# Softmax in one tile of five buffers, with wider lags between the engines and half of the scaling on VectorE

## The chip, the cores and the metric

One core of one Trainium2 chip runs the whole program. The metric is device time in microseconds (us) of one execution. Engine names: PE or TensorE (matmuls and transposes), DVE or VectorE, ACT or ScalarE, SP (DMA issue).

## The reference

One inference step of a two-layer decoder trunk, in fp32, on a prompt of 1024 tokens and a group of 8 samples of 4 new tokens each, with shared weights (model width 1024). Layer 0 is gated linear attention and a ConvFFN. Layer 1 is sliding-window attention (window 128, 16 query heads over 2 key/value heads of width 64, a relative bias per head, one sink per head) and a ConvFFN. Each sub-layer is `h = h + post_norm(f(pre_norm(h)))` with RMSNorm. The attention of layer 1, where the change lies, is

```
s = q @ k.T * 64**-0.5 + bias            # keys of this block and the one before, masked
m = max(max(s), sink)
p = exp(s - m)
denom = sum(p) + exp(sink - m)
o = (p / denom) @ v                      # then o @ w_o_b, the down projection of the stage
```

For the prompt it is computed in blocks of 128 queries against 256 keys. The samples attend to 128 cached keys and their new ones.

## The kernel before

All tokens are transposed: channels lie on the 128 partitions, tokens along the free axis. The 1056 columns are worked on in two halves, X = 0 with 512 columns and X = 1 with 512 prompt and 32 sample columns. Each fp32 product is made of three matmuls, on a rounded part (`hi`) and a remainder (`lo`) of the activations and of the weights. So each weight block of 128x1024 is rounded by ScalarE (L416), its remainder taken by VectorE (L421), in rings of three, and each new activation has a `hi` written by ScalarE and a `lo` by VectorE. SP loads the next raw block when a remainder has been taken.

The stages run one after the other, and within a stage each engine has an order written out by hand; engines meet by counted semaphores alone. The attention stage (`pe_att`, `dve_att`, `act_att`) loops over steps s. A step belongs to one iteration g: a pair of heads (q = g // 4: X and the pair) and one block of 128 queries. There are 64 iterations (NIT), and the loop also carries the rest of the stage, placed by `k, w = divmod(s, 8)`: query projections (`query`, half a block of weights in each of w = 0 to 3), the down projection of the pairs that are complete (`downs`, in w = 4 to 7, a quarter of its 8 or 16 units in each; a unit is the sum over two weight blocks into one of three banks, and VectorE adds it to the accumulator, L471 and L473), the samples' attention (the functions with `s_`, in k = 4 to 8), and two norms whose parts stand in tables by step (`PE_AT`, `DVE_AT`, `ACT_AT`: squares `sq`, folds `f`, the sum over partitions, the root, scaling `s`, residual `a`, then the normed rows `n` and their `hi` and `l`).

One iteration passes these functions, the step at which each engine runs it in brackets:

- `scores(g)` on TensorE [g]: two matmuls into banks 0 and 1. It waits until VectorE has read those of g - 1.
- `biased(g)` on VectorE [g]: adds the bias and finds the maximum with the sink, from the banks into `SS` (two buffers); for the first two of four blocks it also copies the sink's column (L1838).
- `exps(g)` on ScalarE [g]: two exponentials with their sums, from `SS` into `EX` (three buffers).
- `divided(g)` on VectorE [g + 1]: the reciprocal of the two sums.
- `scaled(g)` on ScalarE [g + 1]: two scalings in `EX` by the reciprocals (L1993).
- `transposed(g)` on TensorE [g + 2]: four transposes into bank 2. It waits until ScalarE has copied out those of g - 1.
- `turned(g)` on ScalarE [g + 2]: the copy from bank 2 into `PT` (L2003, L2006).
- `values(g)` on TensorE [g + 3]: the product with the values into a half of bank 4. For an even g it waits for `lo(g - 1)`; in the second half, for g % 8 == 2, also for the sample's new scores (`s_new`), which use the same bank.
- `hi(g)` and `lo(g)`, for an odd g, on ScalarE and VectorE [g + 4]: both blocks of bank 4 into `OH1` and `OL1`, the operands of `downs`.

Within a step the order is: TensorE `scores`, `transposed`, a query half or (w = 4 to 7) `downs` and `s_new`, `values`, `s_scores` and the like, a norm's sum. VectorE: `divided`, `lo`, `biased`, weight remainders, `adds`, the samples' work, the norm's work. ScalarE: `hi`, `scaled`, `exps`, `turned`, `query` (copies and a rounding), roundings, the samples' work, the next bias load, the norm's work. All engines work through their lists in order, so a wait holds everything behind it. A few lines that the prediction speaks of:

```
def biased(g):                                   # VectorE, before
    u, r = g % 2, g % 8
    ...
    dve.wait_ge(sf, g + 1)                       # scores(g)
    if g >= 2:
        dve.wait_ge(es, g - 1)                   # exps(g - 2) has read the buffer
```

Of the kernel before, what the change touches and what calls it, by code (L numbers as in the profile page):

```python
# [15 lines left out]
P = 128  # L16
# [152 lines left out]
def build(nc, wall, xT, gains, ffnpar, wgate, state, kcT, vc, ck, cv, onehot, masks, smask, bmask,  # L169
# [10 lines left out]
    with ctx:  # L180
# [11 lines left out]
        def sem(name):  # L192
# [68 lines left out]
        EX = place("probs", [P, 3, 2, NBW])  # L261
        SS = place("scores", [P, 2, 2, NBW])
# [88 lines left out]
        sn, sk, sf, sa, es, rc, sc = (sem("att_" + x) for x in ("sinks_negated", "sink", "scores", "biased", "exp", "rden", "scaled"))  # L351
        tf, te, of, xh, xl = (sem("att_" + x) for x in ("pt", "pt_copied", "o", "hi", "lo"))
        xsn, xsf, xsa, xsb, xex, xrc, xsc, xtf, xte, xof, xoh, xol = (
            sem("samp_" + x) for x in ("scores_new", "scores", "biased", "masked", "exp", "rden", "scaled", "pt", "pt_copied", "o", "hi", "lo"))
# [1222 lines left out]

        NIT, PAIRS, WINDOWS = 16 * HB, 16, 8
# [10 lines left out]
        def down_bank(k, m):  # L1589
# [8 lines left out]
        DVE_AT = {1: ("f0",), 2: ("f1",), 4: ("s0", "s1"), 5: ("a0", "s2"), 6: ("a1", "s3"), 7: ("a2",), 8: ("a3",), 9: ("F0",),  # L1598
# [4 lines left out]
        PE_AT = {3: "sum", 11: "Sum", 47: "sum", 55: "Sum"}  # L1603
        SUM_BANK = {3: 6, 11: 6, 47: 5, 55: 5}
# [3 lines left out]
        QUERY_DONE = {1: 2, 2: 6} | {q: 8 * ((q - 1) // 2) + (1 if q % 2 else 3) for q in range(3, PAIRS)}  # L1608
# [8 lines left out]
        def pe_att(pe):  # L1617
            def query(q, ks):
# [6 lines left out]
                for c in range(len(CHUNKS[X])):  # L1625
                    if ks[0] == 0 and q:
# [9 lines left out]
                        if q >= 11 and q % 2 and c == 0:  # L1636
                            pe.wait_ge(xsa, 3 * (k - 5) + 3)
                            if q >= 13:
                                pe.wait_ge(ms_done, NORMS[3, "post" if q == 13 else "pre", 0])
# [16 lines left out]
            def transposed(g):  # L1656
                X, q, i, blk, x0 = it_of(g)
                pe.wait_ge(sc, g + 1)
                if g:
                    pe.wait_ge(te, g)  # L1660
                for e in range(2):
                    for k in range(x0 // WIN, 2):
                        m = 2 * e + k
                        last = nc.tensor.transpose(PS[:, 2, m * P:(m + 1) * P], EX[:, g % 3, e, k * WIN:(k + 1) * WIN],
                                                   ident[:])
                last.then_inc(tf, 1)

            def values(g):
                X, q, i, blk, x0 = it_of(g)
                pe.wait_ge(te, g + 1)  # L1670
                if g >= 2 and g % 2 == 0:
                    pe.wait_ge(xl, g // 2)
                    if X and g % 8 == 2:
                        pe.wait_ge(xsa, 3 * (g // 8 - 4) + 1)
# [7 lines left out]
            def downs(k, units):  # L1682
# [3 lines left out]
                if units[0] == 0:  # L1686
# [7 lines left out]
                    else:  # L1694
                        pe.wait_ge(q_ev, AQ[1, min(2 * k - 4, 7), 1])
                for m in units:
# [27 lines left out]
            def s_scores(d, half):  # L1724
                if half:
                    pe.wait_ge(xsa, 3 * d + 2)
# [46 lines left out]
            for s in range(NIT + 4):  # L1773
                k, w = divmod(s, 8)
# [5 lines left out]
                if 2 <= s < NIT + 2:  # L1780
                    transposed(s - 2)
                if k == 0:
                    if w in FIRST_QUERIES:
                        query(*FIRST_QUERIES[w])
                elif w < 2 and k < 8:
                    query(2 * k + 1, (FIRST, SECOND)[w])
                elif w < 4 and k < 7:
# [747 lines left out]
```

## Time and profile before

| | |
|---|---|
| time, median of 3 runs (lowest, highest) | 2627.01 us (2624.51, 2628.49) |
| profiled execution: time, span | 2624.26 us, 2622.5 us |
| mean granted clock of TensorE | 0.983 of full speed |
| instructions | 37815 |
| DMA traffic over the span | 255.18 MB, mean 97 GB/s |

The busy time of an engine is the time in which at least one of its instructions ran. A wait is idle time of an engine before an instruction, put down to the instruction whose semaphore came last; "out<-in" are the program's tile names, and the line is that of the kernel (or of a helper that several places share, as L438 for all projections and L461 for all down projections). The granted clock is a share of full speed: 1.00 stands for 2.4 GHz, and a stretch below it was for a part at 1.2 GHz. The attention stage's first scores start at 1415.17 us, its last (g = 63) at 1783.42 us.

### The profile page before, as it was taken

The page shows a single profiled execution, that of the slowest core. Times are in us where ns is not written, and L with a number is a line of the kernel's source. Part 1 is how long each engine was busy: PE and PEld are TensorE (multiplying, and loading weights), DVE is VectorE, ACT ScalarE, POOL GpSimd, SP SyncE. Part 2 cuts the span into 40 slices and gives each one's busy share as a digit, 9 for nine tenths or more (in the row PEclk, how much of TensorE's full clock was granted, in tenths as well). Part 3 has the DMA queues.
Part 4 walks back from the last instruction along what each step waited for, and adds up shares of the span by engine and source line. Part 5 has one row for each costly group of instructions (what it writes and reads, how often), then busy time and mean ns, then how long its engine had stood idle before and what let it go on. Part 6 is the DMA issues. An engine that isn't in the chain of part 4 may idle for free. (4 is left out here: it accounts for less than half of the span.)

```text
span 2622.5 us, 37815 instructions
## 1 busy us (share of the span) xinstructions
PE 2485.6 (95%) x15455; PEld 2177.1 (83%) x15455; DVE 1619.1 (62%) x2921; ACT 1147.4 (44%) x1810; POOL 0.2 (0%) x4
## 2 busy tenths in 40 slices
PE   7999999999999999999998899989999999999997
PEld 4777989887788889999997676767788889999996
DVE  5677566576666556666655755665666556655556
ACT  4655454453443333343334766663434334332333
POOL 0000000000000000000000000000000000000000
PEclk9999999999999999999999999999999999999998
DMA  4222223223433333322233332231343333332322
GB/s 156 65 73 73 81 84 106 89 91 103 142 113 105 108 99 105 121 93 86 89 95 99 98 97 67 89 100 52 106 139 97 97 96 96 114 113 81 92 86 96
DMA packets 93433, 255.18 MB, mean 97 GB/s; under 512 B 12499, under 2 KB 43708, under 8 KB 91324
## 3 DMA queue, kind: packets, MB, share of 16 engines
q1 hardware_dynamic: 63884, 202.43, 24.4%
q10 hardware_dynamic: 29376, 50.33, 5.8%
q8 instruction: 123, 2.02, 0.3%
q14 instruction: 50, 0.41, 0.1%
HBM read 225.92 MB, written 26.74 MB: 96 GB/s over the span
## 5 line engine op out<-in xcount | busy, mean ns | idle before, releaser
L438 PE MATMUL banks<-act_hi,w_lo 128*128 128x272 f32 (+1 forms) x2952 | 975.0, 330 | 16.8 <-DVE act_lo L2262 7.5
L438 PE MATMUL banks<-act_hi,w_hi 128*128 128x272 f32 (+1 forms) x2952 | 960.9, 326 | 0.0
L438 PE MATMUL banks<-act_lo,w_hi 128*128 128x272 f32 (+1 forms) x2952 | 959.3, 325 | 0.0
L416 ACT ACTIVATE w_hi<-w_raw 128x1024 fp32r<-128x1024 f32 x366 | 380.7, 1055 | 698.3 <-PE banks L461 490.9
L421 DVE TENSOR_TENSOR w_lo<-w_raw,w_hi 128x1024 fp32r<-128x1024 f32 x366 | 442.6, 1223 | 366.3 <-ACT w_hi L416 366.0
L438 PEld LDWEIGHTS banks<-act_hi,w_lo 128*128 128x128 f32 x2952 | 560.2, 190 | 75.2 <-issue 21.3
L438 PEld LDWEIGHTS banks<-act_lo,w_hi 128*128 128x128 f32 x2952 | 561.1, 190 | 43.0 <-issue 1.7
L438 PEld LDWEIGHTS banks<-act_hi,w_hi 128*128 128x128 f32 x2952 | 559.5, 190 | 43.6
L473 DVE TENSOR_TENSOR acc<-acc,banks 128x272 f32<-128x272 f32 (+1 forms) x624 | 315.0, 520 | 191.7 <-PE banks L461 188.2
L461 PE MATMUL banks<-h_hi,w_lo 128*128 128x272 f32 (+1 forms) x1056 | 348.1, 330 | 30.0 <-DVE acc L473 13.1
L461 PE MATMUL banks<-h_hi,w_hi 128*128 128x272 f32 (+1 forms) x1056 | 345.7, 327 | 0.0
L461 PE MATMUL banks<-h_lo,w_hi 128*128 128x272 f32 (+1 forms) x1056 | 345.6, 327 | 0.0
L461 PEld LDWEIGHTS banks<-h_hi,w_lo 128*128 128x128 f32 x1056 | 200.6, 190 | 52.8 <-DVE acc L473 17.3
L461 PEld LDWEIGHTS banks<-h_lo,w_hi 128*128 128x128 f32 x1056 | 202.1, 191 | 16.7
L461 PEld LDWEIGHTS banks<-h_hi,w_hi 128*128 128x128 f32 x1056 | 200.8, 190 | 15.8
L1499 ACT ACTIVATE u<-banks 128x512 f32<-128x512 f32 (+2 forms) x132 | 59.6, 452 | 201.4 <-PE banks L438 198.5
L1513 ACT ACTIVATE c<-u,par 128x512 f32<-128x512 f32 (+1 forms) x88 | 73.1, 830 | 71.0 <-issue 67.9
L1421 DVE SCALAR_TENSOR_TENSOR c<-u,par,c 128x512 f32<-128x512 f32 (+1 forms) x88 | 68.2, 775 | 46.7 <-ACT c L1513 46.7
L1389 DVE TENSOR_TENSOR h_lo<-hf,h_hi 128x512 fp32r<-128x512 f32 (+1 forms) x88 | 62.1, 706 | 34.8 <-ACT h_hi L1554 34.8
L1554 ACT ACTIVATE h_hi<-hf 128x512 fp32r<-128x512 f32 (+1 forms) x88 | 56.0, 637 | 57.5 <-DVE hf L1447 29.9
L461 PE MATMUL banks<-o_hi,w_lo 128*128 128x272 f32 (+1 forms) x192 | 66.6, 347 | 13.4 <-DVE acc L473 8.2
L1845 DVE CUSTOM_DVE_ANT_0 scores<-banks,bias,sinks_b 128x256 f32<-128x256 f32 (+1 forms) x128 | 54.5, 464 | 37.1 <-PE banks L1652 21.9
(231 smaller groups left out, 2591.1 us busy)
## 6 DMA issues: line engine op xcount, KB each, us to landing
w_raw<-wall SPq DMA_DIRECT2D x366, 512.0 KB, 3.6
normed<-h_scratch ACTq DMA_DIRECT2D x20, 352.0 KB, 3.7
h_scratch<-acc ACTq DMA_DIRECT2D x3, 2176.0 KB, 7.6
h_scratch<-acc ACTq DMA_DIRECT2D x3, 2048.0 KB, 8.3
gstates<-state ACTq DMA_DIRECT2D x4, 1024.0 KB, 6.3
gla_s<-gstates ACTq DMA_DIRECT2D x4, 1024.0 KB, 6.6
bias<-bias_scratch ACTq DMA_DIRECT2D x28, 128.0 KB, 2.3
bias_scratch<-bias_rows ACTq DMA_DIRECT2D x8, 383.0 KB
```

The lines of the kernel that those rows point to most:

```text
L416: nc.scalar.activation(WH[:, b % RING], WR[:, b % RAW], ACT.Copy).then_inc(w_hi, 1)
L421: nc.vector.tensor_tensor(WL[:, b % RING], WR[:, b % RAW], WH[:, b % RING].bitcast(fp32), ALU.subtract).then_inc(w_lo, 1)
L438: last = nc.tensor.matmul(PS[:, bank, 0:n], w, a[X][:, k, o:o + n], start=(k == 0 and first), stop=(k == KT - 1 and w is wh and a is AH))
L461: last = nc.tensor.matmul(PS[:, bank, 0:w_], w, a[t][:, o:o + w_], start=(t == 0 and x == 0), stop=(t == 1 and x == 2))
L473: nc.vector.tensor_tensor(a, a, PS[:, bank, 0:w_], ALU.add).then_inc(dn_add, 1)
L1389: nc.vector.tensor_tensor(HL[:, t % 2, 0:W], HF[:, t % 2, 0:W], HH[:, t % 2, 0:W].bitcast(fp32), ALU.subtract).then_inc(hl, 1)
L1421: nc.vector.scalar_tensor_tensor(C[:, 0:cv], U[:, 1:1 + cv], PAR[:, t, 17:18], C[:, 0:cv], ALU.mult, ALU.add).then_inc(cv1, 1)
L1499: last = nc.scalar.activation(U[:, 2 + o:2 + end], PS[:, bank, 0:end - o], ACT.Copy)
L1513: nc.scalar.activation(C[:, 0:cv], U[:, 2:2 + cv], ACT.Identity, bias=PAR[:, t, 19:20], scale=PAR[:, t, 18:19]).then_inc(cb, 1)
L1554: nc.scalar.activation(HH[:, t % 2, 0:WX[X]], HF[:, t % 2, 0:WX[X]], ACT.Copy).then_inc(hh, 1)
L1845: last = nc.vector.tensor_tensor_reduce(SS[:, u, e, x0:2 * WIN], PS[:, e, x0:2 * WIN], BI[:, q % 2, e, x0:], -1.0, SINK[:, 2 * (q % 8) + e ...
```

## The change

The score and probability tiles become one tile `SE` with five buffers; the exponentials and scalings work in place. The lags grow: on ScalarE `exps` at g + 1, `scaled` at g + 3, `turned` at g + 4; on VectorE `divided` at g + 2; on TensorE `transposed` at g + 4, `values` at g + 5; `hi` and `lo` at g + 6. `divided` also scales the second head's probabilities on VectorE, so `scaled` keeps only the first. The sink's column is copied for each iteration (its buffer is now overwritten by the exponential). `k, w` are counted from s - 1. On TensorE `values` and `s_new` come before `downs`, whose units are spread 1, 3, 2, 2 (X = 0) and 2, 5, 4, 5 (X = 1) over the four steps. On VectorE `divided` comes behind `biased`, and `s_new` is one step later. The norm tables move, the sums of the second norm use bank 3, and the first projection of the next layer is cut differently. The semaphore of the sample's biased scores is split in two.

```diff
-        EX = place("probs", [P, 3, 2, NBW])
-        SS = place("scores", [P, 2, 2, NBW])
+        SE = place("scores", [P, 5, 2, NBW])
...
         ACT_AT = {0: ("sq0",), 1: ("sq1",), 2: ("h0", "h1"), 3: ("root",), 5: ("h2",), 6: ("h3",), 8: ("Sq0",), 9: ("Sq1",),
-                  11: ("Root",), 12: ("hi0",), 14: ("hi1",),
-                  38: ("sq0",), 39: ("sq1",), 41: ("h0", "h1"), 47: ("root",), 50: ("h2",), 51: ("h3",), 52: ("Sq0",), 53: ("Sq1",),
-                  55: ("Root",), 57: ("hi0",), 60: ("hi1",)}
+                  11: ("Root",), 12: ("hi0",), 15: ("hi1",),
+                  39: ("sq0",), 40: ("sq1",), 42: ("h0", "h1"), 43: ("root",), 46: ("h2",), 47: ("h3",), 51: ("Sq0",),
+                  53: ("Sq1",), 57: ("Root",), 58: ("hi0",), 60: ("hi1",)}
...
-                  10: ("F1",), 12: ("n0a", "n0b"), 13: ("l0a", "l0b"), 14: ("n1a", "n1b"), 15: ("l1a", "l1b"),
-                  39: ("f0",), 40: ("f1",), 48: ("s0",), 49: ("s1",), 50: ("a0", "s2"), 51: ("a1", "s3"), 52: ("a2", "a3"),
-                  53: ("F0",), 54: ("F1",), 56: ("n0a",), 57: ("n0b",), 58: ("l0a", "l0b"), 59: ("n1a",), 60: ("n1b",),
-                  61: ("l1a",), 62: ("l1b",)}
-        PE_AT = {3: "sum", 11: "Sum", 47: "sum", 55: "Sum"}
-        SUM_BANK = {3: 6, 11: 6, 47: 5, 55: 5}
+                  10: ("F1",), 12: ("n0a", "n0b"), 13: ("l0a", "l0b"), 15: ("n1a", "n1b"), 16: ("l1a", "l1b"),
+                  40: ("f0",), 41: ("f1",), 44: ("s0", "s1"), 45: ("a0",), 46: ("a1",), 48: ("s2",), 49: ("s3",),
+                  50: ("a2", "a3"), 52: ("F0",), 54: ("F1",), 58: ("n0a", "n0b"), 59: ("l0a", "l0b"),
+                  60: ("n1a", "n1b"), 61: ("l1a",), 62: ("l1b",)}
+        PE_AT = {3: "sum", 11: "Sum", 43: "sum", 57: "Sum"}
+        SUM_BANK = {3: 6, 11: 6, 43: 3, 57: 3}
...
+        UNITS = ((0, 1, 4, 6, 8), (0, 2, 7, 11, 16))
...
-            for s in range(NIT + 4):
-                k, w = divmod(s, 8)
+            for s in range(NIT + 5):
+                k, w = divmod(s - 1, 8)
...
-                if 2 <= s < NIT + 2:
-                    transposed(s - 2)
+                if 4 <= s < NIT + 4:
+                    transposed(s - 4)
...
+                if w == 5 and 0 <= d < 4:
+                    s_new(d)
+                if 5 <= s < NIT + 5:
+                    values(s - 5)
                 if w >= 4 and 1 <= k < 8:
-                    units = len(down_units((k - 1) // 4)) // 4
-                    downs(k - 1, range((w - 4) * units, (w - 3) * units))
-                if d >= 0 and w == 4 and d < 4:
-                    s_new(d)
-                if 3 <= s < NIT + 3:
-                    values(s - 3)
+                    downs(k - 1, units_at(k - 1, w))
...
             def biased(g):
-                u, r = g % 2, g % 8
-                if i < 2:
-                    if g >= 2:
-                        dve.wait_ge(es, g - 1)
-                    p = q % 8
-                    nc.vector.tensor_copy(SS[:, u, :, 2 * WIN:NBW], SINK[:, 2 * p:2 * p + 2].unsqueeze(2)).then_inc(sk, 1)
+                u, r, p = g % 5, g % 8, q % 8
+                if g >= 5:
+                    dve.wait_ge(tf, g - 4)
+                else:
+                    dve.wait_ge(sf, g + 1)
+                nc.vector.tensor_copy(SE[:, u, :, 2 * WIN:NBW], SINK[:, 2 * p:2 * p + 2].unsqueeze(2)).then_inc(sk, 1)
...
                 nc.vector.reciprocal(ST[:, g % 8, 6:8], ST[:, g % 8, 4:6]).then_inc(rc, 1)
+                dve.wait_ge(rc, g + 1)
+                x = SE[:, g % 5, 1, x0:2 * WIN]
+                nc.vector.tensor_scalar(x, x, ST[:, g % 8, 7:8], None, ALU.mult).then_inc(sc1, 1)
...
-                for e in range(2):
-                    x = EX[:, g % 3, e, x0:2 * WIN]
-                    last = nc.scalar.activation(x, x, ACT.Copy, scale=ST[:, g % 8, 6 + e:7 + e])
-                last.then_inc(sc, 1)
+                x = SE[:, g % 5, 0, x0:2 * WIN]
+                nc.scalar.activation(x, x, ACT.Copy, scale=ST[:, g % 8, 6:7]).then_inc(sc, 1)
...
-                if s >= 4 and s % 2 == 1:
-                    hi(s - 4)
+                if s >= 7 and s % 2:
+                    hi(s - 6)
                 if 1 <= s <= NIT:
-                    scaled(s - 1)
-                if s < NIT:
-                    exps(s)
-                if 2 <= s < NIT + 2:
-                    turned(s - 2)
+                    exps(s - 1)
+                if 3 <= s < NIT + 3:
+                    scaled(s - 3)
+                if 4 <= s < NIT + 4:
+                    turned(s - 4)
```

## Rows read from the trace of the kernel before

**Rows 1.** The page's first part: busy time and share of each engine.
```profile
...
PE 2485.6 (95%) x15455; PEld 2177.1 (83%) x15455; DVE 1619.1 (62%) x2921; ACT 1147.4 (44%) x1810; POOL 0.2 (0%) x4
...
```

**Rows 2.** Busy time by stretch: stretch, length, each engine's busy us, granted clock.
```profile
...
1415.00:1499.00 84.00, 64.05 (x356) 43.81 (x356) 56.04 (x140) 62.57 (x135) 0.00 (x0) 0.96 0.31 101
1499.00:1593.00 94.00, 88.24 (x553) 68.43 (x555) 53.38 (x138) 58.48 (x152) 0.00 (x0) 0.96 0.34 96
1593.00:1812.00 219.00, 198.32 (x1511) 156.63 (x1508) 129.26 (x353) 137.21 (x332) 0.00 (x0) 0.97 0.24 75
...
```

**Rows 3.** Waits of TensorE, 1400 to 1805 us: total us, times, longest.
```profile
...
PE banks L1664 <- ACT probs_t L2006: 14.4, 11, 2.8
PE banks L461 <- DVE acc L473: 8.3, 6, 2.8
PE banks L1678 <- DVE o_lo L1859: 7.4, 5, 2.5
PE banks L1678 <- DVE s_scores L1874: 3.3, 4, 1.0
PE banks L461 <- DVE w_lo L421: 3.2, 2, 1.8
...
PE banks L1664 <- ACT probs_t L2003: 2.6, 1, 2.6
...
```

**Rows 4.** Busy time by 10 us stretch; the third last column is the clock.
```profile
...
1440.00:1450.00 10.00, 7.75 (x43) 5.27 (x43) 9.72 (x22) 7.52 (x25) 0.00 (x0) 0.83 0.30 82
...
1790.00:1800.00 10.00, 10.00 (x61) 7.77 (x61) 4.20 (x8) 5.47 (x10) 0.00 (x0) 0.83 0.33 106
...
```

**Rows 5.** Timeline of all engines, step 13 of the stage: start us, us.
```profile
...
1478.87 2.86 DVE L568 SCALAR_TENSOR_TENSOR normed<-acc,gain_cols,rstd 128x544 f32<-128x544 f32 x4
...
1479.38 0.66 PE L1664 MATMUL banks<-ident,probs 128*128 128x128 f32 x4
...
1481.77 2.02 ACT L578 ACTIVATE act_hi<-normed 128x2176 fp32r<-128x2176 f32 x1 [2.79 <-DVE normed L568]
...
1483.69 0.36 ACT L2015 ACTIVATE o_hi<-banks 128x256 fp32r<-128x256 f32 x1
...
1484.09 0.42 DVE L1859 TENSOR_TENSOR o_lo<-banks,o_hi 128x256 fp32r<-128x256 f32 x1 [2.28 <-ACT o_hi L2015]
...
1484.66 0.66 PE L1678 MATMUL banks<-probs_t,v_tok 128*64 128x128 f32 x8 [1.82 <-DVE o_lo L1859]
...
```

**Rows 6.** Timeline of all engines, step 37 of the stage.
```profile
...
1617.85 0.70 PE L1652 MATMUL banks<-kg,q 64*128 64x256 f32 x4
...
1618.60 0.48 DVE L1845 CUSTOM_DVE_ANT_0 scores<-banks,bias,sinks_b 128x256 f32<-128x256 f32 x1 [0.71 <-PE banks L1652]
...
1622.57 0.18 DVE L1874 TENSOR_TENSOR s_scores<-banks,s_bias 128x32 f32<-128x32 f32 x1
1622.66 0.68 DVE L1880 TENSOR_TENSOR s_scores<-banks,s_bias 128x512 f32<-128x512 f32 x1
...
1622.90 0.66 PE L1678 MATMUL banks<-probs_t,v_tok 128*64 128x128 f32 x8 [0.97 <-DVE s_scores L1874]
...
1623.49 1.07 PE L1732 MATMUL banks<-kcg,q_sample 64*64 64x512 f32 x4
...
```

**Rows 7.** Groups by shape, 1405 to 1800 us: busy us, mean ns | idle.
```profile
...
L1993 ACT ACTIVATE probs<-probs,stats 128x256 f32<-128x256 f32 x112 | 50.5, 500 | 27.0 <-DVE stats L1852 24.1 <-issue 2.8
L1845 DVE CUSTOM_DVE_ANT_0 scores<-banks,bias,sinks_b 128x256 f32<-128x256 f32 x112 | 49.5, 480 | 27.6 <-PE banks L1652 21.9 <-issue 5.7
...
L416 ACT ACTIVATE w_hi<-w_raw 128x1024 fp32r<-128x1024 f32 x33 | 33.9, 1051 | 11.7 <-PE banks L461 11.7
...
L1852 DVE RECIPROCAL stats<-stats 128x2 f32<-128x2 f32 x64 | 10.3, 160 | 16.3 <-ACT probs L1984 16.1
...
```

**Rows 8.** Timeline of VectorE in the sample's scaling.
```profile
...
1637.65 0.17 DVE L1898 RECIPROCAL s_stats<-s_stats 128x1 f32<-128x1 f32 x1
1637.86 0.77 DVE L1900 TENSOR_SCALAR s_scores<-s_scores,s_stats 128x1056 f32<-128x1056 f32 x1
...
```

More of the change, by code:

```diff
@@ L1663, in transposed @@
                         m = 2 * e + k
-                        last = nc.tensor.transpose(PS[:, 2, m * P:(m + 1) * P], EX[:, g % 3, e, k * WIN:(k + 1) * WIN],
+                        last = nc.tensor.transpose(PS[:, 2, m * P:(m + 1) * P], SE[:, g % 5, e, k * WIN:(k + 1) * WIN],
                                                    ident[:])
@@ L1695, in downs @@
                         pe.wait_ge(q_ev, AQ[1, min(2 * k - 4, 7), 1])
+                    if k in (4, 6):
+                        pe.wait_ge(ms_done, NORMS[3, "post" if k == 4 else "pre", 0])
                 for m in units:
@@ L1814, in pe_att @@
                     pe.wait_ge(sa, NIT)
-                elif s == NIT + 2:
+                elif s == NIT + 4:
                     pe.wait_ge(te, NIT)
-                if s >= NIT:
-                    pe_first_block(pe, 2, "u" if w < 2 else "val", (FIRST, SECOND)[w % 2])
+                    pe_first_block(pe, 2, "val", ALL)
+                if NIT <= s < NIT + 4:
+                    pe_first_block(pe, 2, "u", range(2 * (s - NIT), 2 * (s - NIT) + 2))
             downs(7, range(len(down_units(1))))
@@ L1908, in s_lo @@
                 last.then_inc(xol, 1)
-            for s in range(NIT + 4):
-                k, w = divmod(s, 8)
+            for s in range(NIT + 6):
+                k, w = divmod(s - 1, 8)
                 d = k - 4
-                if 1 <= s <= NIT:
-                    divided(s - 1)
-                if s >= 4 and s % 2 == 1:
-                    lo(s - 4)
+                if s >= 7 and s % 2:
+                    lo(s - 6)
                 if s < NIT:
                     biased(s)
+                if 2 <= s < NIT + 2:
+                    divided(s - 2)
+                if w == 6 and 0 <= d < 4:
+                    s_new(d)
                 for q in range(1, PAIRS):
@@ L1923, in dve_att @@
                     rest_after(dve, ("kv", 1, w // 2 - 1))
-                elif w == 0 and k >= 2:
-                    for t in range(2):
-                        rest_after(dve, ("ao", (k - 2) // 4, (k - 2) % 4, t))
+                elif w < 2 and k >= 2:
+                    rest_after(dve, ("ao", (k - 2) // 4, (k - 2) % 4, w))
                 if w >= 4 and 1 <= k < 8:
-                    units = len(down_units((k - 1) // 4)) // 4
-                    adds(k - 1, range((w - 4) * units, (w - 3) * units))
+                    adds(k - 1, units_at(k - 1, w))
                 if d >= 0:
@@ L2064, in act_att @@
             act.wait_ge(cn_out, 16)
-            for s in range(NIT + 4):
-                k, w = divmod(s, 8)
+            for s in range(NIT + 6):
+                k, w = divmod(s - 1, 8)
                 d = k - 4
-                if s >= 4 and s % 2 == 1:
-                    hi(s - 4)
+                if s >= 7 and s % 2:
+                    hi(s - 6)
                 if 1 <= s <= NIT:
-                    scaled(s - 1)
-                if s < NIT:
-                    exps(s)
-                if 2 <= s < NIT + 2:
-                    turned(s - 2)
+                    exps(s - 1)
[3 more added lines that the diff above has]
+                    turned(s - 4)
                 for q in range(1, PAIRS):
@@ L2078, in act_att @@
                         query(q)
-                if w == 7 and k:
+                if w == 7 and k > 0:
                     downs_done(k - 1)
@@ L2096, in act_att @@
                         act_step(act, *pass_at(s), name, SUM_BANK.get(s))
-                if s in (20, 23):
-                    act_hi(act, 2, "mix", 1, (s - 20) // 3)
+                if s in (21, 24):
+                    act_hi(act, 2, "mix", 1, (s - 21) // 3)
             for what in ("u", "val"):
```

71 lines of the change are left out of this document (36 added, 35 removed).

## The prediction

> **What bounds the kernel now.** I read the page's first part, then the busy time by stretch, the waits of TensorE, the durations by shape, and the timelines around three waits. TensorE is busy for 95% of the span [rows 1], so outside the attention stage there is nothing for this change to win. The change touches one stage, from about 1415 us to 1812 us. There TensorE is busy for 64.1 of 84, 88.2 of 94 and 198.3 of 219 us [rows 2]: 350.6 of 397 us, so about 46 us of idle time. VectorE is busy for 238.7 us and ScalarE for 258.3 us of the same 397 us. No engine is full, and the idle time of TensorE comes from hand-overs. The reader should see by name what those 46 us are [rows 3]: 14.4 + 2.6 us before a transpose that waits until ScalarE has copied the previous block's transposed probabilities out of the one bank; 8.3 us before a down-projection unit that waits for VectorE's accumulation; 3.2 us for a weight remainder; 7.4 us before the value product that waits for VectorE's `lo` of the pair before; 3.3 us before the value product that waits for the sample's new scores. That is 39.2 us. The clock is the other loss: there are eight dips of it in the stage, each like the 10 us stretches at a granted clock of 0.83, the first from 1440 and the last from 1790 [rows 4]. In each, TensorE was at the lower level (1.2 GHz) for part of the stretch after having waited, and a 10 us stretch at 0.83 does 1.7 us less work. What lies in those stretches is partly hidden behind the other engines.
>
> **The change part by part.** All sums are against the profiled execution's own time, 2624.3 us (a span of 2622.5 us and 1.8 us around it); the median of the runs shown is 2.8 us above it, and I add that at the end.
>
> *Later transposes and no same-step exponentials (first term).* Before, ScalarE's copy in a step stands behind that step's exponentials, which stand behind VectorE's biased scores, which stand behind TensorE's scores of the same step. After, exponentials lag by one step, the scaling by three, the copy by four. That removes the ping-pong of 17.0 us [rows 3] where nothing else holds ScalarE. It does not remove it where ScalarE sits in the norm's squares, its root or its 2.02 us `act_hi` [rows 5], because the transpose of one step still needs the copy of the step before, at the same distance as now. The longest of these waits are such ones. I let 5 us go; the ends are 0 and 17.
>
> *Units spread 1, 3, 2, 2 and 2, 5, 4, 5, and the second norm's residual work spread over more steps (second term).* The 8.3 + 3.2 us before down-projection units arise where VectorE is behind in its queue. Fewer units in the first of the four steps and less norm work beside them let most of it go. The sample's masking stays where it was. I take 8 us off; the ends are 0 and 11.5.
>
> *The value product moves ahead of the down-projection units (third term, the largest).* In a step with units the order on TensorE was scores, transposes, units, values; it becomes scores, transposes, values, units. The value product of an even block waits for `lo` of the odd block before it, which comes from `hi` on ScalarE, which comes from the value product one step earlier. The lag is wider, but `hi` and `lo` are shifted so that they stay in the step of that value product. Until now units covered the hand-over. Without them TensorE reaches the values after at most 0.70 us of scores [rows 6] and 0.66 us of transposes [rows 5]; the two overlap a little, and I reckon 1.05 to 1.3 us. In the first step with units ScalarE first finishes the query that ended just before, whose copies are followed by a weight rounding of 1.051 us [rows 7]; then come `hi` 0.36 us and `lo` 0.42 us [rows 5]. That is 1.8 us, the copies and two hand-overs beside it. The stall is an estimated 1 to 2 us; it appears in three windows (in the later ones the sample's value products lie in between): 5 us. It is worse behind `act_hi`. In step 13 of the kernel before, the chain normed 2.86 us, `act_hi` 2.02 us, `hi`, `lo` ended 1.82 us after TensorE was ready, although two units had just run [rows 5]. Those two units would now stand behind the wait; they filled the time from the transposes at 1479.38, 0.66 us long, to 1482.84, where the wait began: 2.8 us. So such a place costs about 4.6 us, and there are three: steps 13, 59 and 61, since `act_hi` is placed in 12, 58 and 60. That makes 14 us, with 5 us above and about 1.5 us elsewhere, against 7.4 us now: +13 us. The ends are −7 (all of it hidden) and +18.
>
> *The sample's new scores one step later (fourth term).* VectorE's add now stands behind the biased scores and the scaling of the same step, and TensorE's value product of that step waits for it. From the start of TensorE's scores VectorE begins 0.75 us later [rows 6], needs some 0.9 us for its two biased rows of 0.48 us [rows 7] (they overlap a little), about 0.5 us for reciprocal and scaling (below) and 0.18 us for the add: 2.4 us with the hand-over. TensorE is there after 1.05 to 1.3 us. So 1.1 to 1.4 us in each of four windows, 5.3 us against 3.3 us now [rows 3]: +2 us, ends −3.3 and +5.
>
> *The second half of the sample scores (fifth term).* It waits for VectorE's 0.68 us add of the first half. Now the value product lies between [rows 6]: the add begins at 1622.66, the second half starts at 1623.49, right behind the values. When the values are gone from there, TensorE waits through the accumulation of the last unit and that add, 1.3 to 1.5 us, four times: +5.5 us, ends 0 and +6.
>
> *The second head's scaling on VectorE (sixth term).* ScalarE loses 56 operations of 0.500 us and 8 shorter ones [rows 7], some 30 us of its time. VectorE gains 64 scalings. The trace has none of this shape; the nearest rows are the 1056-wide one at 0.77 us [rows 8] and the two-column reciprocal at 0.160 us [rows 7], which are the ends, and a line through both gives 0.31 us, the value I take. In front of it VectorE waits for its own reciprocal: in the sample's chain the scaling starts 0.21 us behind the reciprocal's start [rows 8]. With 32 more two-column sink copies (each about the 0.160 us of the reciprocal) VectorE gets 64 × 0.31 + 32 × 0.16 = 25 us more, 264 of 397 us: hidden behind TensorE as a whole. Where VectorE leads, in the first steps, it is not: +1.5 us, ends 0 and +6. What queues behind that new wait is the rest of VectorE's step: weight remainders, accumulations, norm work. The scaling in place and the shared tile change no shape.
>
> *Edits at nothing.* The first projection of the next layer in four quarters and then whole is the same work in the drain, where its matmuls cover the longer tail of transposes and values. The sums' new bank and the split semaphores add no instruction on a path. The weight queue follows VectorE's remainders by the same wait as now, and ScalarE's rounding never waited for a load in this stage (the 11.7 us of idle time in its row are TensorE's) [rows 7].
>
> The sum: −5 − 8 + 13 + 2 + 5.5 + 1.5 = +9 us, with the clock's dips left at eight. On the profiled execution that is 2633.3 us; with the 2.8 us to the median, **2636 us**, slower by 0.34%. A change under about 0.2%, 5.3 us, can't be told from none by measuring this kernel.
>
> **Rivals.** *The lag works (faster).* ScalarE idles 27.0 us before the scalings alone [rows 7], because they wait within the step. Relieved of half of them and with every input a step old, it may run ahead, so that `hi` starts the moment the value product ends. The rival decides where `hi`, `lo` and two hand-overs, about 1 us, fit under scores and transposes, 1.05 to 1.3 us as above. Then the third to fifth terms come to about zero, the first to −12 and the second to −9: 2624.3 − 21 + 2.8 = 2606 us. For it: the gap is that narrow. Against it: the query's rounding stands ahead of `hi` on ScalarE.
>
> *The waits trade places (no change).* If VectorE's norm chain ends some 3 us earlier than now at each of the three places, the third term falls from +13 to about +4 and the sum to 0: 2627 us. For it: the first norm's root is no longer behind exponentials of its own step. Against it: the chain starts with squares that wait for VectorE, which has more to do.
>
> *The clock follows the waits (slower still).* About nine of the new stalls are over 1 us long. If each is answered by one more stretch like those in [rows 4], 1.7 us apiece, the time is 2636 + 15 = 2651 us. Against it: of some thirty waits now only eight are followed by a dip. The Trainium skill, "TensorE: Matmul & The Clock Gate", section "HAM oscillation — how this bites in real kernels", describes a kernel whose bursts of matmuls each start cold after a wait, and says that the transition cost is paid for every burst instead of once. By that rule this rival would hold; the trace agrees only in part, with dips behind eight of the waits.
>
> **How the numbers follow.** The forecast gets 0.36, with a range of its own from 2632.5 to 2643 us; the faster rival 0.33; no change 0.22; the clock 0.09. Cases of both signs hold most of the chance, so the full range reaches from 2602 to 2653 us: a little below the faster rival, where the first term gives more, and just above the clock's. Faster by over 0.2%: 0.33. Within: 0.22. Slower: 0.36 + 0.09 = 0.45.
>
> **What would show it.** In the profile after, the waits of value products for `lo` should grow from 7.4 to about 20 us, above all at steps 13, 59 and 61; those for the sample's scores to 5 us, with a new one of 5 us at the second half. Waits for transposed probabilities should fall only to about 12 us and those for accumulations to 3 or 4 us. VectorE's busy time should rise by 20 to 30 us, ScalarE's fall by 26 to 31 us. The forecast is wrong if value products hardly wait; then the faster rival stands.

## The result, and the profile after

The changed kernel takes 2636.5 us (median of 9 runs, 2630.9 to 2639.1) against 2624.5 us of the kernel before (9 runs, 2620.5 to 2629.5): a ratio of 1.004 with an interval of 1.003 to 1.005. The forecast was 2636 us. Its profiled execution took 2631.8 us, a span of 2629.9 us. The first part of the page, answering to [rows 1]:

```profile
PE 2488.9 (95%) x15455; PEld 2176.6 (83%) x15455; DVE 1642.5 (62%) x3017; ACT 1119.8 (43%) x1746; POOL 0.2 (0%) x4
```

VectorE gained 23.4 us of work, ScalarE lost 27.6 us, and TensorE has as many matmuls as before. What changed is when TensorE waits. Its waits from 1400 to 1840 us, answering to [rows 3] (total us, times, longest):

```profile
PE banks L1686 <- DVE o_lo L1870: 23.9, 12, 4.9
PE banks L1672 <- ACT probs_t L2011: 5.6, 2, 3.3
PE banks L1686 <- DVE s_scores L1885: 5.4, 4, 2.2
PE banks L1742 <- DVE s_scores L1891: 4.8, 4, 1.4
...
PE banks L1672 <- ACT probs_t L2014: 2.8, 1, 2.8
PE banks L461 <- DVE w_lo L421: 2.0, 1, 2.0
...
PE banks L461 <- DVE acc L473: 1.3, 3, 0.6
PE banks L461 <- DVE acc L471: 0.2, 1, 0.2
```

The reader should see two groups. The waits that were large in [rows 3], for `probs_t` and `acc`, are small. In their place stands one row, `o_lo`, 7.4 us before and 23.9 us now, with two smaller ones for the sample's scores. The view of before has one more wait for `acc`, which the prediction did not count:

```profile
PE banks L461 <- DVE acc L471: 2.1, 1, 2.1
```

Step 13 shows how the wait for `o_lo` comes about (timeline of all engines, answering to [rows 5]):

```profile
1465.13 2.87 DVE L568 SCALAR_TENSOR_TENSOR normed<-acc,gain_cols,rstd 128x544 f32<-128x544 f32 x4 [1.08 <-ACT rstd L523]
...
1467.12 0.66 PE L1672 MATMUL banks<-ident,scores 128*128 128x128 f32 x4
...
1468.07 2.01 ACT L578 ACTIVATE act_hi<-normed 128x2176 fp32r<-128x2176 f32 x1
1469.98 0.37 ACT L2023 ACTIVATE o_hi<-banks 128x256 fp32r<-128x256 f32 x1
...
1470.38 0.43 DVE L1870 TENSOR_TENSOR o_lo<-banks,o_hi 128x256 fp32r<-128x256 f32 x1 [2.38 <-ACT o_hi L2023]
...
1470.95 0.69 PE L1686 MATMUL banks<-probs_t,v_tok 128*64 128x128 f32 x4 [3.18 <-DVE o_lo L1870]
```

TensorE has nothing to do after the transposes of 1467.12 until `lo` is there: `hi` stands behind the 2.01 us of `act_hi` on ScalarE. The down units, which filled that time before, come after the values (e1 below shows what they would do in this place now).

The whole stage, from the first scores to the last down unit's matmul, in both kernels (busy time by stretch: length, busy us of each engine, granted clock). First before, then after:

```profile
1415.17:1822.88 407.71, 360.83 (x2496) 279.02 (x2495) 245.68 (x644) 258.27 (x617) 0.00 (x0) 0.97 0.27 84
```

```profile
1409.41:1831.07 421.66, 368.99 (x2496) 283.73 (x2495) 269.42 (x740) 230.66 (x553) 0.00 (x0) 0.95 0.26 81
```

The stage is 14.0 us longer. TensorE's idle time in it rose by 5.8 us, from 46.9 to 52.7, and its busy time by 8.2 us although the matmuls are the same: the granted clock fell from 0.97 to 0.95. Summed over windows of 1 us, TensorE stood at the lower level (1.2 GHz) for 27.3 us before and 40.9 us after; half of the difference, 6.8 us, is about what the lost speed costs. The lowest stretches, answering to [rows 4] (10 us each):

```profile
1440.00:1450.00 10.00, 7.16 (x38) 5.08 (x38) 7.57 (x22) 6.75 (x20) 0.00 (x0) 0.66 0.70 244
...
1470.00:1480.00 10.00, 9.05 (x37) 6.10 (x38) 7.89 (x20) 5.75 (x20) 0.00 (x0) 0.66 0.19 54
1770.00:1780.00 10.00, 7.36 (x44) 5.16 (x44) 4.95 (x18) 5.87 (x14) 0.00 (x0) 0.66 0.01 2
```

The last two hold the ends of the waits of step 13 (at 1470.95) and step 61 (at 1772.64). (The execution as a whole is only 7.6 us longer than the one before, because its stage began 5.8 us earlier. Nothing ahead of the stage was changed, and the stage begins anywhere from 1409.4 to 1418.5 us in the fourteen profiled executions of this study.)

### The profile page after: what moved, and what is told of

Same layout as the page of the kernel before. It is cut to its first block and busy times, and to the rows that moved or that the text cites. A ratio compares the mean times of both kernels' runs of the same rounds, so it can differ in the third digit from the quotient of the medians.

```text
span 2629.9 us, 37807 instructions
## 1 busy us (share of the span) xinstructions
PE 2488.9 (95%) x15455; PEld 2176.6 (83%) x15455; DVE 1642.5 (62%) x3017; ACT 1119.8 (43%) x1746; POOL 0.2 (0%) x4
## 5 line engine op out<-in xcount | busy, mean ns | idle before, releaser
L438 PE MATMUL banks<-act_hi,w_lo 128*128 128x272 f32 (+1 forms) x2952 | 975.3, 330 | 16.3 <-DVE act_lo L2271 7.1
L461 PE MATMUL banks<-go_hi,w_lo 128*128 128x272 f32 (+1 forms) x192 | 62.7, 326 | 9.2 <-issue 6.0
```

The costliest lines, as they stand in the source:

```text
L438: last = nc.tensor.matmul(PS[:, bank, 0:n], w, a[X][:, k, o:o + n], start=(k == 0 and first), stop=(k == KT - 1 and w is wh and a is AH))
L461: last = nc.tensor.matmul(PS[:, bank, 0:w_], w, a[t][:, o:o + w_], start=(t == 0 and x == 0), stop=(t == 1 and x == 2))
```

## The experiments

All are timed in five rounds beside the kernel before, whose median was 2624.9 to 2625.2 us in them. The stage, idle time and low clock are of each one's profiled execution, measured as above. One execution can lie well off its kernel's median: e4's took 2644.8 us, the changed kernel's 2631.8 and e15's 2613.3.

| kernel | median us | ratio to before (interval) | stage us | TensorE idle us | at 1.2 GHz us |
|---|---|---|---|---|---|
| before | 2624.5 | 1 | 407.7 | 46.9 | 27.3 |
| after | 2636.5 | 1.004 (1.003 to 1.005) | 421.7 | 52.7 | 40.9 |
| e1 values late | 2623.5 | 0.9997 (0.9986 to 1.0007) | 407.5 | 42.8 | 37.6 |
| e2 scaling on ScalarE | 2640.1 | 1.006 (1.0048 to 1.0072) | 426.0 | 53.8 | 47.8 |
| e3 sample's add early | 2634.8 | 1.0036 (1.0024 to 1.0048) | 420.8 | 49.0 | 47.8 |
| e4 `act_hi` later | 2637.0 | 1.0051 (1.0038 to 1.0065) | 425.7 | 54.6 | 44.4 |
| e5 = e1 + e3 | 2621.5 | 0.9988 (0.9975 to 1.0001) | 404.9 | 41.9 | 34.1 |
| e7 even units | 2639.4 | 1.0061 (1.0042 to 1.0081) | 424.7 | 54.5 | 41.0 |
| e8 `lo` a step earlier | 2651.0 | 1.0109 (1.0083 to 1.0135) | 434.3 | 61.3 | 51.2 |
| e9 = e8 + sample early | 2639.7 | 1.0059 (1.0039 to 1.0079) | 425.5 | 51.2 | 58.1 |
| e12 before, values early | 2665.8 | 1.0148 (1.0119 to 1.0176) | 451.5 | 73.9 | 68.3 |
| e13 old residual pass | 2641.1 | 1.0063 (1.0038 to 1.0089) | 426.1 | 56.7 | 37.6 |
| e14 = e5 + old pass | 2620.4 | 0.9976 (0.9962 to 0.999) | 406.0 | 40.1 | 37.6 |
| e15 = e14 + scaling on ScalarE | 2620.4 | 0.9982 (0.997 to 0.9994) | 403.5 | 41.4 | 27.3 |

**e1, values behind the down units again.**

```diff
-                if 5 <= s < NIT + 5:
-                    values(s - 5)
                 if w >= 4 and 1 <= k < 8:
                     downs(k - 1, units_at(k - 1, w))
+                if 5 <= s < NIT + 5:
+                    values(s - 5)
```

> The changed kernel with values(s - 5) behind the down units again in TensorE's step; all else stays. Theory (the waits for lo are what the change bought with its new order, 23.9 us of them at L1686): the down units of the step, 3.5 to 7 us, stand before values again, so the waits for o_lo fall to about 8 us, the waits for the new scores' addition (5.4 us) lie behind the down units too and go, and the clock loses fewer low stretches; the time falls 15 to 20 us below the changed kernel, to 2617 to 2622 us, some 5 us below the kernel before. Rival 'VectorE's scaling delays lo': the waits stay at 16 us or more and the time stays within 4 us of 2636.5. Rival 'waits trade places': the waits for accumulations, gone in the changed kernel, come back with 8 us or more, and the time falls by less than 10 us.

Measured: 2623.5 us, 13 us under the changed kernel, where 15 to 20 were expected, and the same as the kernel before. The mechanism is the theory's only in part. Its waits (same view):

```profile
PE banks L461 <- issue: 14.1, 6, 5.0
PE banks L1686 <- DVE o_lo L1870: 6.0, 4, 3.7
...
PE banks L1742 <- DVE s_scores L1891: 2.4, 4, 0.8
...
```

`o_lo` fell to 6.0 us, and the waits of 5.4 us for the new scores are gone, as foretold. But 14.1 us appeared at the down units, put down to "issue". Step 13 in e1's timeline tells what that is:

```profile
1476.42 0.37 ACT L2023 ACTIVATE o_hi<-banks 128x256 fp32r<-128x256 f32 x1
...
1476.82 0.42 DVE L1870 TENSOR_TENSOR o_lo<-banks,o_hi 128x256 fp32r<-128x256 f32 x1 [2.38 <-ACT o_hi L2023]
...
1477.45 0.47 PE L461 MATMUL banks<-o_hi,w_lo 128*128 128x512 f32 x1 [3.24 <-issue]
```

The unit starts 0.21 us behind the end of `lo`, and so do the other five of these waits (0.21 to 0.24 us). The code says why: `downs(k - 1, ...)` begins with a wait for `xl` up to 4k, that is `lo(8k - 1)`. That `lo` is now taken in step 8k + 5, in which the units begin; before it was taken in step 8k + 3 and the units began in 8k + 4. So in the first step with units the units can cover nothing: they ask for the same `lo`. This was not in the prediction. Of 23.9 us the order gives back 3.8 (6.0 + 14.1 remain); the new scores' 5.4 and half of the second half's 4.8 go as well. With other waits a little longer TensorE idles 9.9 us less, and its busy time in the stage is 4.3 us shorter, of which 1.7 us are half of the 3.3 us less at the lower level. So of the order's 13 us `lo` is the smaller part.

**e12, the new order alone.** In the kernel before, values and the sample's new scores move ahead of the units; VectorE's add of the new scores moves ahead of its accumulations.

```diff
+                if d >= 0 and w == 4 and d < 4:
+                    s_new(d)
+                if 3 <= s < NIT + 3:
+                    values(s - 3)
                 if w >= 4 and 1 <= k < 8:
                     ...
-                if d >= 0 and w == 4 and d < 4:
-                    s_new(d)
-                if 3 <= s < NIT + 3:
-                    values(s - 3)
```

> The kernel before with one thing of the change alone: TensorE's values (and the sample's new scores) stand ahead of the down units; VectorE takes the new scores ahead of its adds, without which this order could not run. Theory (the order of values and down units is what cost the 13 us, whatever the lag and the buffers): the waits for o_lo rise from 7.4 to 14 to 20 us, the new scores' addition from 3.3 to about 5, and the time from 2625 to 2632 to 2640. Rival 'the lag of two steps is the cause, the order matters only with it': o_lo stays under 10 us and the time within 3 us of 2625. Rival 'values early bring the next step's lo and copies forward': the waits for probs_t and the accumulation fall by 5 us or more, and the time falls.

Measured: 2665.8 us, 41 us over before, far more than expected. Its waits:

```profile
PE banks L1678 <- DVE o_lo L1859: 34.5, 10, 5.9
PE banks L1664 <- ACT probs_t L2007: 9.4, 6, 2.5
PE banks L1678 <- DVE s_scores L1874: 8.9, 4, 4.3
PE banks L1732 <- DVE s_scores L1880: 4.8, 4, 1.4
...
```

Here the order alone takes the wait for `lo` from 7.4 to 34.5 us. The stage grew by 43.7 us: 27.0 of idle time and 16.7 of busy time, where half of the 41.0 us more at the lower level would be 20.5. The order costs 41 us without the rest of the change and 13 us with it. So the rest (buffers, lags, units, norm tables and scaling together) wins some 28 us where values stand early, and nothing that can be told where they stand late (e1 against before: 0.9997).

**e8, `hi` and `lo` at the end of the values' own step.** If `lo` is late because it starts a step after its values, starting it earlier should help.

```diff
-                if s >= 7 and s % 2:
-                    lo(s - 6)
 ...
+                if s >= 6 and s % 2 == 0:
+                    lo(s - 5)
                 if w >= 4 and 1 <= k < 8:
                     adds(k - 1, units_at(k - 1, w))
```

The same for `hi` on ScalarE, behind the query's copies.

> The changed kernel with hi and lo of a pair of queries taken at the end of the step in which TensorE makes the pair's second values (hi(s - 5) on ScalarE behind the step's copies, lo(s - 5) on VectorE ahead of the adds), and not at the start of the next; all else stays, values ahead of the down units too. Theory (lo is taken one step after its values, behind whatever the residual's pieces leave on ScalarE and VectorE, and both the next values and the group's first down units ask for it in that same step): the waits for o_lo fall from 23.9 to 6 us or less, the first down units wait for nothing, the long low stretches of the clock at the first and last residual passes shrink, and the time falls by 18 to 26 us, to 2610 to 2619. Rival 'ScalarE and VectorE now stand still in line': both wait for TensorE's values inside the step, so the probabilities and the accumulators come later; the waits for probs_t, stats and acc rise by 10 us or more and the time stays above 2630. Rival 'only the order on TensorE counts': waits move, time within 4 us of 2636.5.

Measured: 2651.0 us, 14 us slower. The first rival holds:

```profile
PE banks L1672 <- ACT probs_t L2014: 12.2, 6, 2.8
PE banks L1659 <- DVE stats L1852: 10.5, 7, 2.8
PE banks L461 <- DVE acc L473: 7.7, 4, 3.7
PE banks L1686 <- DVE o_lo L1870: 5.3, 5, 1.5
...
PE banks L461 <- DVE acc L471: 3.5, 2, 2.9
...
```

`o_lo` fell to 5.3 us as expected, and other waits rose by more: `probs_t` from 8.4 to 16.3 us (with the 4.1 us of another row), `stats` from 3.7 to 10.5, `acc` from 1.5 to 11.2. VectorE itself now stands idle for 79.6 us before `lo`, waiting for `hi`, against 51.8 us in the changed kernel, and what is queued behind `lo` is late. Taking `lo` earlier only chooses another victim.

**e4, `act_hi` later.** `hi0` in steps 13 and 59 instead of 12 and 58, the last `hi1` in 61, their `lo` pieces a step later.

```diff
-                  11: ("Root",), 12: ("hi0",), 15: ("hi1",),
+                  11: ("Root",), 13: ("hi0",), 15: ("hi1",),
 ...
-                  53: ("Sq1",), 57: ("Root",), 58: ("hi0",), 60: ("hi1",)}
+                  53: ("Sq1",), 57: ("Root",), 59: ("hi0",), 61: ("hi1",)}
```

> The changed kernel with the residual's hi0 taken one step later (13 and 59), the last layer's hi1 at 61, and their lo steps one step later with them, so that ScalarE does no 2-us residual piece in the steps 12 and 58 to 60 in which hi and the sums' copies are due for lo. Theory (the three long waits of values at steps 13, 59 and 61, 11.8 us together, come of the residual's act_hi of 2 us ahead of o_hi on ScalarE): two of the three at least fall under 1.5 us, o_lo's waits from 23.9 to 14 to 17 us, and the time falls by 6 to 10 us, to 2626 to 2631. Rival 'lo is late everywhere': the long waits move to other steps (15, 61, 63) with the piece, the sum stays above 21 us and the time within 2 us of 2636.5.

Measured: 2637.0 us; `o_lo` 22.1 us. The waits at 13 and 59 fell, 3.18 to 1.29 and 3.70 to 1.91 us, but 2.39 us came up at step 15, and step 61 stayed at 5 us with another cause (its timeline):

```profile
1782.05 2.74 DVE L568 SCALAR_TENSOR_TENSOR normed<-acc,gain_cols,rstd 128x512 f32<-128x512 f32 x4
...
1784.71 0.42 DVE L1870 TENSOR_TENSOR o_lo<-banks,o_hi 128x256 fp32r<-128x256 f32 x1
1784.82 1.91 ACT L578 ACTIVATE act_hi<-normed 128x2048 fp32r<-128x2048 f32 x1 [3.34 <-DVE normed L568]
...
1785.27 1.13 PE L1686 MATMUL banks<-probs_t,v_tok 128*64 128x128 f32 x8 [5.01 <-DVE o_lo L1870]
```

Now VectorE's own norm holds `lo`, and `act_hi` comes after. The rival is right; the theory, that `act_hi` alone makes the wait, is not. (The edit has a part in step 61: its later `lo` pieces of the norm stand ahead of the norm's rows in step 60 on VectorE.)

**e3, the sample's first add ahead of the accumulations**; **e5, that with e1**; and **e9, that with e8, and the new scores' add right behind `lo` in w = 5 (before: in w = 6).**

```diff
+                if w == 5 and d >= 0:
+                    s_add(d, 0)
                 if w >= 4 and 1 <= k < 8:
                     adds(k - 1, units_at(k - 1, w))
 ...
-                    elif w == 5:
-                        s_add(d, 0)
```

> The changed kernel with s_add(d, 0) ahead of the down units' adds in VectorE's steps w = 5; all else stays. Theory (the second half of the sample's scores waits for an addition that is queued behind the adds): the four waits at L1742 go from 1.1 to 1.4 us each to under 0.3, 4.8 us to 1 us or less, and the time falls by 3 to 5 us, to 2631 to 2634. Rival 'the wait moves on': the adds come 0.6 us later, and lo or the accumulations of the same steps wait by as much; the time stays within 1.5 us of 2636.5.

Measured: 2634.8 us. The waits at L1742 are gone (4.8 us), those for the new scores rose by 1.0 and for `o_lo` by 0.9, and TensorE idles 3.7 us less. The median fell by 1.7 us, which the intervals do not separate from nothing.

> The changed kernel with values behind the down units (as in e1) and s_add(d, 0) ahead of the adds (as in e3). Theory (what is left at L1742 with values late, 2.4 us in e1, goes, and nothing takes its place): 1 to 3 us under e1's 2623.5, so 2620.5 to 2622.5; the waits of the first down units for lo (13 us) stay as in e1. Rival: the same as e1 within 1 us.

Measured: 2621.5 us, 2.0 under e1, with overlapping intervals. The waits at L1742 are gone here too; those for `o_lo` at the values rose from 6.0 to 7.6 us.

> As e8, and VectorE takes the sample's new scores (s_new) right behind that lo in step w = 5 and the first half of the sample's scores (s_add(d, 0)) ahead of the adds. Theory: beside what e8 gives, the 5.4 us at L1686 for s_scores and the 4.8 us at L1742 go to 1.5 us or less together; 7 to 9 us under e8, so 2602 to 2611. Rival 'the waits move on': the adds and lo come later by what was moved ahead of them, the accumulation waits rise by as much, and the time is within 3 us of e8's.

Measured: 2639.7 us, 11.2 us under e8 (intervals apart). Both kinds of sample waits are gone from the view, 5.0 + 4.8 us in e8, and the others stayed within 2 us of e8's. So these two waits do cost what they last, in this pair; the absolute forecast failed with e8's.

**e7, even units.** 

```diff
-        UNITS = ((0, 1, 4, 6, 8), (0, 2, 7, 11, 16))
+        UNITS = ((0, 2, 4, 6, 8), (0, 4, 8, 12, 16))
```

> The changed kernel with the down units spread evenly over their four steps (2, 2, 2, 2 and 4, 4, 4, 4 in place of 1, 3, 2, 2 and 2, 5, 4, 5), which is the spread of the kernel before. Theory (term 2 of the prediction: the uneven spread takes away the waits for the accumulation): the accumulation's waits (L473, L471) rise from 1.5 to 6 to 11 us and the time by 4 to 9 us, to 2640 to 2646. Rival 'it was the residual's spread, not the units'': the accumulation's waits stay under 3 us, and the time stays within 2 us of 2636.5. Rival 'a longer first portion covers lo' is excluded by the order, since values stand ahead of the units.

Measured: 2639.4 us, not separable from the changed kernel. The accumulation's waits are 1.3 + 0.2 us as in it. The uneven spread is not what took them away.

**e13, the second residual pass placed as before**, and **e14, that with e5.**

```diff
-        PE_AT = {3: "sum", 11: "Sum", 43: "sum", 57: "Sum"}
+        PE_AT = {3: "sum", 11: "Sum", 48: "sum", 56: "Sum"}
```

ScalarE's and VectorE's pieces of that pass go with it, and the wait for the bank's reader goes back from the units to the query.

> The changed kernel with the second residual pass (steps 39 to 63) placed as in the kernel before, each piece one step later than there because the steps are counted from 1 now, its two sums in the bank of the sample's scores again. Theory (term 2: the pass's new spread, and not the down units', takes away the waits for the accumulation): the accumulation's waits rise from 1.5 to 6 us or more, the time to 2640 to 2646. Rival 'the new spread makes the long waits': the pieces that stand ahead of o_hi in steps 58 and 60 (act_hi 1.9 us, normed 2.7 us) are split, the waits for o_lo at steps 59 and 61 fall from 8.6 to 5 us or less, and the time falls by 3 to 6 us, to 2630 to 2634.

Measured: 2641.1 us. Both sides are in its waits:

```profile
PE banks L1688 <- DVE o_lo L1870: 17.0, 12, 3.2
PE banks L1688 <- DVE s_scores L1885: 7.0, 4, 3.8
...
PE banks L461 <- DVE acc L473: 5.1, 4, 2.8
...
PE banks L438 <- ACT rstd L521: 4.2, 2, 2.1
...
```

`acc` rose by 3.8 us and 4.2 us for the root came back; `o_lo` fell by 6.9, at steps 59 and 61 from 8.6 to 3.4. The pass's spread moves waits about and gains nothing that shows.

> As e13, but with values behind the down units and s_add(d, 0) ahead of the adds (as in e5). Theory of term 2: 3 to 8 us over e5's 2621.5, so 2625 to 2630, with the accumulation's waits back. Rival as in e13: the first down units' wait at step 61 (5.0 us in e1 and e5) and o_lo's at 59 (3.7) fall by 4 us together, and the time falls to 2616 to 2619, under both kernels.

Measured: 2620.4 us, 1.1 under e5, not separable from it; the ratio lies below 1 with its whole interval. Against e5, the 5.0 us wait of step 61 became 1.3 and the 3.7 us of step 59 2.2; `acc` is at 5.9 us and the root at 2.6.

**e2, both heads' scaling on ScalarE**, and **e15, the same in e14.**

```diff
-                x = SE[:, g % 5, 0, x0:2 * WIN]
-                nc.scalar.activation(x, x, ACT.Copy, scale=ST[:, g % 8, 6:7]).then_inc(sc, 1)
+                for e in range(2):
+                    x = SE[:, g % 5, e, x0:2 * WIN]
+                    last = nc.scalar.activation(x, x, ACT.Copy, scale=ST[:, g % 8, 6 + e:7 + e])
+                last.then_inc(sc, 1)
```

VectorE's scaling goes, and with it TensorE's wait for it.

> The changed kernel with both heads' probabilities scaled by ScalarE (as before the change); VectorE does the reciprocal alone. Theory (the scaling stands beside the bound, and its place is not what costs): VectorE's busy time falls by about 23 us, ScalarE's rises by about 27, the waits for o_lo stay between 19 and 26 us, and the time stays within 3 us of the changed kernel's 2636.5. Rival 'VectorE is the bound at the waits': o_lo's and the sample scores' waits fall by 8 us or more together and the time by 8 to 12 us, to about 2626. Rival 'ScalarE had no room': the transposes wait for the scaling again, 8 us more of L1672, and the time rises by 5 to 10.

Measured: 2640.1 us; VectorE's busy time 21.8 us lower, ScalarE's 23.7 higher, `o_lo` 24.0 us as in the changed kernel. The medians differ by 3.6 us, but the intervals of the two ratios just overlap.

> As e14, but ScalarE scales both heads' probabilities again (as in e2). Theory (VectorE's scaling is a gain of some 3 us by itself, as e2's 2640.1 against 2636.5 suggests, since ScalarE's 0.4 to 0.5 us less a step bring the probabilities earlier): 2 to 5 us over e14's 2620.4, so 2622 to 2625, with the waits for probs_t up by 2 us or more. Rival 'the scaling's place is worth nothing': within 1.5 us of e14. Rival of the prediction's term 6 (VectorE's 25 us more of work delay the adds and cost 1.5 us): 1 to 2 us under e14.

Measured: 2620.4 us, the same as e14. Where the scaling is done is worth nothing there that shows; in the changed kernel VectorE's scaling may be a gain of some 3 us, which is not shown.

## Why the prediction was right

The time was right, and so was the largest term, to 3.5 us; of its reasons only a part was. By its steps, on the two profiled executions:

- *First term* (−5): the waits of transposes for the copy fell from 17.0 us to 8.4 (5.6 + 2.8): −8.6. No run takes the lags alone away, so that they did it is argued and not shown.
- *Second term* (−8): the waits before the units were 11.5 us by the prediction's two rows [rows 3], and 13.6 with the 2.1 us of L471 that it left out; they became 3.5: −10.1. Of its two reasons e7 excludes the units' spread, and e13, the residual's old place, brings back 3.8 us of accumulation waits. The rest is not explained by a run.
- *Third term* (+13): 7.4 to 23.9 us: +16.5. Steps 13, 59 and 61 waited 3.2, 3.7 and 4.9 us, against 4.6 us foretold; the others came to 12.1 us, where 6.5 us were reckoned. The size is about right, but the reason given, that the units no longer cover the hand-over, accounts for little of it. With the units in front again (e1), 20.1 of the 23.9 us remain: 6.0 at the values, and 14.1 at the group's first units, which ask for the same `lo` in the same step and wait as long as the values had waited there. So against the kernel before, 12.7 of the 16.5 us come with the rest of the change and 3.8 with the order. In the kernel before, where the units did cover it, the order alone makes +27.1 us (e12). Either edit takes the cover away; the prediction saw one of them, and that its sum still fits is luck. Step 59 was listed for the wrong reason: it has no units in either kernel, and e1 keeps its 3.7 us. And e4 shows that `act_hi` is not the one cause: the norm's pieces on both engines delay whatever is queued behind them.
- *Fourth and fifth term* (+2 and +5.5): +2.1 (3.3 to 5.4) and 4.8 from nearly nothing. In e9 removing both was worth 11 us beside e8; in the changed kernel removing the fifth alone gave 1.7 us, not separable from nothing (e3).
- *Sixth term* (+1.5): the scaling took 0.355 us, where 0.31 was estimated, and VectorE gained 23.4 us for 25. A cost is not shown: moving it back gave +3.6 us (e2) and 0.0 (e15).

```profile
L1863 DVE TENSOR_SCALAR scores<-scores,stats 128x256 f32<-128x256 f32 x56 | 19.9, 355 | 2.0
```

That is the group by shape after, from 1400 to 1820 us (busy us, mean ns, idle ahead of it), the row that the kernel before did not have.

- *The clock* (left at eight dips): in the profiled executions the dips are nine, three of them twice as long as the others, and some 7 to 8 of the stage's 14.0 us are theirs (half of the low time 6.8, all of the busy time 8.2). That term, put at nothing, was mis-sized, and it is the rival "the clock follows the waits" at half its price. One execution says little here, though: e14 and e15 have the same median, and their profiled executions, of 2623.0 and 2613.3 us, had 37.6 and 27.3 us of low clock. Over the six kernels that keep the change's order with `lo` in place (after, e2, e3, e4, e7, e13) idle time is 53.5 us on average, low clock 43.3 and the stage 424.2; over the five with values late (before, e1, e5, e14, e15) 42.6, 32.8 and 405.9. Of the 18.3 us between them 10.9 are waits and about 5 are clock by the half of the low time; some 2 are not accounted for. The Trainium skill, "TensorE: Matmul & The Clock Gate", section "HAM oscillation — how this bites in real kernels", describes a kernel in which every burst after a wait pays the transition again; here the rows agree in direction, but not for each wait: the changed kernel has 35 waits in the whole of the view above and nine dips.

So of the foretold waits, −5 − 8 + 13 + 2 + 5.5 = +7.5 us, +4.7 us came (−8.6 − 10.1 + 16.5 + 2.1 + 4.8), the errors of the first two terms and the third cancelling in part. With waits that the prediction did not price, such as 1.5 us for a copy of the query (L1978), TensorE's idle time rose by 5.8 us; its busy time rose by 8.2 us, where the prediction had nothing, and the two make the stage's 14.0. Between the medians the difference is 12.0 us, where 9 were foretold; that 2636 met 2636.5 so closely is luck, since these 3 us are made up for by the median of before, which over 9 runs came out 2.5 us below the 2627.0 us that the forecast was built on.

The rival "the lag works" fails at the third term, as its condition said it would: `hi` does not start when the values end, since the queue of ScalarE holds other work (in step 13, `act_hi` until 1469.98 us). "The waits trade places" is the one that the experiments bring up again and again (e4, e8, e13), though not at the change itself.

What stays open: why one execution has eight dips of the clock and another eleven, whether the scaling's place is worth the 3.6 us of e2 or nothing, as in e15, and what the lags alone are worth. The obvious next step, the down units one step later so that they do not ask for a `lo` of their own step, was not tried.

The best kernel of the study is the changed one with values late, the sample's add early and the old pass (e14, e15): 0.24% and 0.18% under the kernel before, 0.6% under the changed one. Of the change, e15 keeps little more than the buffers, the lags and the units' spread.

## What to carry to other kernels

When two waits for the same hand-over sit in one step, putting independent work between them helps only if that work does not ask for the same thing: look up what every instruction behind the wait waits for itself. A wait that shrinks when a piece of another engine's queue is moved comes up elsewhere unless the piece gets shorter or finds idle time; so count the sum over all waits, not the row that was aimed at. A deeper lag has to move every reader of what is handed over: here `hi` and `lo` moved with the values, but the units came to ask for the same `lo` in the same step, and where the old order had covered that hand-over the rest of the change won nothing that shows (e1).

## What the runs showed of the hardware

TensorE's busy time less half of its time at 1.2 GHz is nearly the same in all fourteen kernels, 343 to 351 us in the stage (before 347.2, after 348.5, e12 343.4), while the stage itself goes from 403.5 to 451.5. So, to within these 8 us, a low stretch costs about half its length in all of them, and the rest of the differences is idle time. Waits alone do not set the low time: e3 idles 49.0 us and e13 56.7 us, with 47.8 and 37.6 us at the lower level.
